# A one-layer hybrid trunk on one core: VectorE makes the last doubling of the scan's rotation, and GpSimd's pool sums wait twice

## The chip, the core and the metric

The kernel runs on one core of a Trainium2 chip. A core has five engines with queues of their own: TensorE (PE, matrix products into PSUM banks), VectorE (DVE), ScalarE (ACT), GpSimd (POOL), and SyncE (SP), which here only issues DMAs. They meet in semaphores: an instruction adds to one when it is done, and a queue can wait until one has reached a count. The metric is the device time of one execution in microseconds, lower is better.

## The reference

For 512 tokens of width 1024 (float32):

```
z = x @ w_in                       # split: pool 256, q k v 3 x 384, ssm 384
pool : mean of the last 2/4/8/16 tokens minus the token, per group @ w_pool, * pool_scale
attn : 6 heads of 64, causal by chunks of 64, clipped relative-position bias, softmax
ssm  : 24 groups of 16 channels, 64 complex states each:
       s[t] = abar * s[t-1] + bbar @ u[t];  y = Re(c @ s) + d * u
       y = gelu(y);  y = y * sigmoid(y @ w_glu + b_glu)      # the gated unit
h    = LayerNorm(alpha*x + concat(rmsnorm(pool), rmsnorm(attn), rmsnorm(ssm)) @ w_out)
ffn  = top-2 of 16 experts (silu(h@w_gate) * (h@w_up)) @ w_down, inside the best group of 4
ple  = sigmoid(h @ w_ple_gate) * (p @ w_ple_proj)
x    = LayerNorm(alpha*h + ffn + ple)
```

The change touches the state space group (ssm) and the pool group.

## The kernel before

The program is written out by hand, one queue for each engine; what stands in a queue runs in that order, and no scheduler moves anything. Many fp32 products are made as three products of rounded parts: an upper part (ScalarE copies into fp32r), and a lower part (VectorE or GpSimd subtracts the upper one). `xv_lo` (value input), `wv_lo` (value weights), `gelu_lo` and `wg_lo` (gated unit) are such lower parts.

**The scan.** The 512 tokens are cut into 64 chunks (NC) of 8 tokens. TensorE makes each chunk's contribution x (`products`, signal `pe_x`) into four PSUM banks, for 12 pairs of groups (Q) of 128 states by 64 chunks, real and imaginary. The complex scan over the chunks is made real by a rotation: VectorE multiplies x by the turned unit vectors `cosv` and `sinv` (L1697 to L1706), scans real and imaginary parts with the real decay (L1708), and rotates back (L1716 to L1721), which signals `s_ready`. The rotation table `rot` holds the powers 0 to 64 of a unit vector, and **GpSimd** makes it by doubling: with powers 1 to m at hand, powers m+1 to 2m are these times power m, a complex product of six instructions (L557 to L562), for m = 1, 2, 4, 8, 16, 32. Then it writes the decay array (L565, L566), which signals the third `rot_ready`, and VectorE waits for that.

**GpSimd's queue** goes on behind it: 16 DMA issues that put half of the matrix `m0` together (L575; SP issues the other half), the first running sums of the pool group (`add_shift`, L583 and L584), `xv_lo` in two subtractions (L594), and, once VectorE has put y and the skip term together (`yin_ready`), the longer sums, a multiply by the reciprocal counts (L602, `rcnt`) and a subtract of the token (L603), which signals `pool_ready`. For this TensorE's pool product (L1258), ScalarE's squares and one of SP's loads wait. `gelu_lo` is made by VectorE at L1758 (`glu_lo_set`, with the weights' part before it: 4 in all); TensorE's gated unit (L1219 to L1221) waits for all four, ScalarE's gates (L814) for it.

**VectorE's queue** around it: bias and row maximum of heads 0 and 1, the wait, the rotation and scan, `normalise(0)` and `normalise(1)` (a reciprocal, then four multiplies of a softmax block, L1676, signal `p_norm`), bias of heads 2 and 3 (L1656, L1658; for `scores(1)` of TensorE), their maxima (L1667), the same for heads 4 and 5, `wv_lo`, the other normalisations, then y (L1747), copies of transposed probabilities (`pt_move`, L1752) and `gelu_lo`. **TensorE's queue**: x, two q/k projections, half of the pool projection, scores(1), the first value tile, scores(2) (waits for the bias of heads 2 and 3, `s_read` 4), y, the second value tile (its second term takes `xv_lo`, its third `wv_lo`), transposes of the probabilities, more value tiles, the gated unit, the pool product, attention times values, the output product. **ScalarE** makes the exponentials (L767) and copies y out of PSUM (L822).

Of the kernel before, what the change touches and what calls it, by code (L numbers as in the profile page):

```python
# [23 lines left out]
P = 128  # L24
# [10 lines left out]
NC = T // CH  # L35
# [82 lines left out]
def trunk(nc, io, out):  # L118
    with ExitStack() as ctx:
# [384 lines left out]
        def _(gp):  # L504
            n = [0]

            def link(ins):

                n[0] += 1
                ins.then_inc(S["gp_step"], 1)  # L510
                gp.wait_ge(S["gp_step"], n[0])
# [25 lines left out]
            link(g.tensor_copy(rot[:, 0, :, 1:2], u8[:, 0, :].unsqueeze(2)))  # L537
            link(g.tensor_copy(rot[:, 1, :, 1:2], u8[:, 1, :].unsqueeze(2)))
            m = 1
            while m < NC:  # L540
                if m == 8:
                    gp.wait_ge(S["rb_in"], 16)
                    g.memset(rbias[0:64, :, 192:256], NEG).then_inc(S["rot_ready"], 1)
                    for i in range(4):
                        h, f = i % 2, i // 2
                        gp.dma_start(w_pl[64 * h:64 * h + 64, f, 64 * h:64 * h + 64], io["w_pool"][i]).then_inc(S["gp_in"], 16)
                    gp.dma_start(inv_d.rearrange("(p c) o -> p (c o)", p=P), pad_t[:]).then_inc(S["inv_put"], 16)
                    gp.wait_ge(S["pe_qk"], 4)
                    g.memset(m0, 0.0).then_inc(S["rot_ready"], 1)
                    gp.wait_ge(S["kern_in"], 4)  # L550
                shape = [P, Q, m]
                t = tmp_g[:, 0:Q * m].rearrange("p (q c) -> p q c", q=Q)
                ar, ai = rot[:, 0, :, 1:m + 1], rot[:, 1, :, 1:m + 1]
                br = rot[:, 0, :, m:m + 1].broadcast_to(shape)
                bi = rot[:, 1, :, m:m + 1].broadcast_to(shape)
                orr, oi = rot[:, 0, :, m + 1:2 * m + 1], rot[:, 1, :, m + 1:2 * m + 1]
                link(g.tensor_tensor(t, ai, bi, ALU.mult))  # L557
                link(g.tensor_tensor(orr, ar, br, ALU.mult))
                link(g.tensor_tensor(orr, orr, t, ALU.subtract))
                link(g.tensor_tensor(t, ar, bi, ALU.mult))  # L560
                link(g.tensor_tensor(oi, ai, br, ALU.mult))
                link(g.tensor_tensor(oi, oi, t, ALU.add))  # L562
                m *= 2
# [12 lines left out]

            gp.wait_ge(S["pool_in_done"], 2)
            gp.wait_ge(S["pe_x"], 1)
            a, b2 = pl_s[:, 0], pl_s[:, 1]

            def add_shift(o, i, w, lo, ms):
# [17 lines left out]
            link(g.tensor_copy(b2[64:P, 1:2], a[64:P, 1:2]))  # L599
            add_shift(a, b2, 8, 64, second)  # L600
            gp.wait_ge(S["rc_in"], 16)
            link(g.tensor_tensor(a, a, rcnt, ALU.mult))  # L602
            g.tensor_tensor(a, a, plT, ALU.subtract).then_inc(S["pool_ready"], 1)  # L603

# [922 lines left out]
        def _(dv):  # L1527
# [153 lines left out]
            row_max(0)  # L1681
            row_max(1)

            dv.wait_ge(S["pe_x"], 1)
            dv.wait_ge(S["rot_ready"], 3)
            half = Q // 2 * NC
            cosv, sinv = rot[:, 0, :, 0:NC], rot[:, 1, :, 0:NC]

            def qc(ap):
                return ap.rearrange("p (q c) -> p q c", c=NC)  # L1690
            for u in range(2):
                xr, xi = qc(bank[X_BANKS[0][u]][:, 0:half]), qc(bank[X_BANKS[1][u]][:, 0:half])
                cs, sn = cosv[:, 6 * u:6 * u + 6], sinv[:, 6 * u:6 * u + 6]
                cols = slice(u * half, (u + 1) * half)
                o_r, o_i = qc(x_rot[:, 0, cols]), qc(x_rot[:, 1, cols])
                t_r, t_i = qc(x_tmp[:, 0, cols]), qc(x_tmp[:, 1, cols])
                link(tt(o_r, xr, cs, ALU.mult))  # L1697
                link(tt(t_r, xi, sn, ALU.mult))
                link(tt(o_i, xi, cs, ALU.mult))
                last = tt(t_i, xr, sn, ALU.mult)  # L1700
                if u == 0:
                    link(last)
# [435 lines left out]
```

## Time and profile before

| | before |
|---|---|
| median of 3 runs | 423.56 us (422.49 to 425.38) |
| profiled execution, time | 422.09 us |
| its span | 420.3 us |
| PE busy | 407.8 us (97%) |
| DVE busy | 260.9 us (62%) |
| ACT busy | 143.8 us (34%) |
| POOL busy | 115.5 us (27%) |
| chain that ended last | PE 47%; DVE 29%; issue 11%; DMA 5%; POOL 4%; ACT 3% |

TensorE is busy nearly all the time, but in the first half by small pieces that wait on the other engines; the second half is the experts. The chain that ended last is read back from the last instruction, at each step to what released it. Idle time of an engine counts only where such a chain goes through it. The row of a timeline may merge several instructions of a line; then its length is that of all of them, and its shape that of the first.

### The profile page before, as it was taken

How to read it: one execution, taken by the hardware profiler on the slowest of the kernel's cores; microseconds unless marked ns; L12 is line 12 of the kernel's file. 1: busy time of each engine (PE TensorE's matmuls, PEld its weight loads, DVE VectorE, ACT ScalarE, POOL GpSimd, SP SyncE). 2: the span in 40 equal slices, each digit the busy share in tenths (PEclk: the TensorE clock that was granted, in tenths of full speed). 3: DMA queues.
4: the chain of work that ended last, by engine and by line, in shares of the span. 5: the costliest groups of instructions: out<-in, count | busy, mean ns of one | idle time of the engine just before them, and what ended most of it. 6: DMA issues, size and time to landing. Idle time of an engine off the chain costs nothing.

```text
span 420.3 us, 5727 instructions
## 1 busy us (share of the span) xinstructions
PE 407.8 (97%) x2213; PEld 246.0 (59%) x2213; DVE 260.9 (62%) x467; ACT 143.8 (34%) x254; POOL 115.5 (27%) x142
## 2 busy tenths in 40 slices
PE   8999999999999999999999999999999999999992
PEld 5767755459987557888587876333333333333281
DVE  2999994999884999999988323111110112224986
ACT  4732236248757891214520101011111011111284
POOL 2811258457054706000001640011101111000050
PEclk9999999999999999999999999999999999999998
DMA  7994103350579995111763239999999999978204
GB/s 269 430 403 139 50 2 62 74 131 27 132 294 343 397 409 202 50 51 50 271 281 105 95 85 387 423 394 423 420 419 419 417 412 409 423 279 299 101 13 188
DMA packets 33643, 102.77 MB, mean 245 GB/s; under 512 B 14898, under 2 KB 16098, under 8 KB 26832
## 3 DMA queue, kind: packets, MB, share of 16 engines
q1 hardware_dynamic: 26048, 92.79, 56.8%
q0 software_dynamic: 4016, 7.97, 5.6%
q10 hardware_dynamic: 3552, 1.65, 1.4%
q8 instruction: 18, 0.29, 0.3%
q14 instruction: 9, 0.07, 0.1%
HBM read 93.29 MB, written 15.24 MB: 258 GB/s over the span
## 4 chain that ended last, share of the span: by engine, by line
PE 47%; DVE 29%; issue 11%; DMA 5%; POOL 4%; ACT 3%; SPq 0%; DVEq 0%; POOLq 0%; ACTq 0%
PE bank L1392 20%; PE bank L1402 10%; DVE region_f L1812 4%; PE bank L1387 3%; PE bank L1227 3%; PE bank L1467 3%; PE bank L1143 2%; POOL slot_scratch L631 1%; DMA region_h<-y_scratch 1%; ACT region_a L767 1%; DVE ln_st L1815 1%; DVE region_a L1658 1%; DVE region_a L1676 1%; DVE att_mx L1667 1%; DMA region_h<-slot_scratch 1%
## 5 line engine op out<-in xcount | busy, mean ns | idle before, releaser
L1392 PE MATMUL bank<-region_a,region_g 128*64 128x512 f32 (+1 forms) x224 | 77.8, 594 | 0.0
L1974 DVE TENSOR_TENSOR region_c<-region_c,bank 128x256 f32<-128x256 f32 x12 | 5.1, 421 | 64.7 <-ACT region_c L962 64.7
L1402 PE MATMUL bank<-region_a,region_c 128*64 128x512 f32 (+1 forms) x160 | 43.7, 596 | 0.0
L1392 PE MATMUL bank<-region_h,region_g 128*64 128x512 f32 (+1 forms) x96 | 42.4, 594 | 0.0
L1392 PE MATMUL bank<-region_c,region_g 128*32 128x512 f32 (+1 forms) x96 | 42.4, 595 | 0.0
L1392 PE MATMUL bank<-region_b,region_g 128*64 128x512 f32 (+1 forms) x96 | 42.4, 594 | 0.0
L1967 DVE COPY region_g<-bank 128x512 f32<-128x512 f32 x24 | 15.4, 686 | 40.6 <-PE bank L1387 40.6
L1392 PEld LDWEIGHTS bank<-region_a,region_g 128*64 128x64 f32 (+1 forms) x224 | 22.2, 123 | 25.1 <-issue 24.4
L962 ACT ACTIVATE region_c<-bank 128x256 f32<-128x256 f32 x12 | 4.6, 384 | 83.9 <-PE bank L1392 83.9
L1013 PE MATMUL bank<-region_e,region_a 128*128 128x512 f32 x64 | 28.0, 595 | 0.0
L1320 PE MATMUL bank<-ple_gate_upper,hidden_upper 128*128 128x512 f32 x64 | 25.7, 402 | 0.0
L1322 PE MATMUL bank<-ple_gate_upper,hidden_lower 128*128 128x512 f32 x64 | 25.0, 390 | 0.0
L1321 PE MATMUL bank<-ple_gate_lower,hidden_upper 128*128 128x512 f32 x64 | 24.9, 389 | 0.0
L1402 PEld LDWEIGHTS bank<-region_a,region_c 128*64 128x64 f32 (+1 forms) x160 | 12.0, 123 | 22.1 <-issue 22.0
L644 POOL DMA_INDIRECT expert_scratch<-region_g,region_h x5 | 5.0, 1001 | 65.1 <-ACT region_g L945 65.1
L1402 PE MATMUL bank<-region_c 128*32 128x512 f32 (+1 forms) x48 | 21.9, 596 | 0.0
L1402 PE MATMUL bank<-region_b,region_c 128*64 128x512 f32 (+1 forms) x48 | 21.7, 595 | 0.0
L1013 PEld LDWEIGHTS bank<-region_e,region_a 128*128 128x128 f32 x64 | 12.0, 190 | 14.6 <-issue 14.3
L907 ACT ACTIVATE region_h<-bank 128x512 f32<-128x512 f32 x8 | 4.8, 598 | 41.8 <-PE bank L1322 30.3
L1392 PEld LDWEIGHTS bank<-region_h,region_g 128*64 128x64 f32 (+1 forms) x96 | 11.4, 123 | 12.5 <-issue 12.2
L1812 DVE SCALAR_TENSOR_TENSOR region_f<-bank,rms_r,region_f 128x512 f32<-128x512 f32 x24 | 18.0, 750 | 0.7
L631 POOL DMA_INDIRECT slot_scratch<-region_h,slot_i x8 | 8.2, 1027 | 36.4 <-issue 36.4
(380 smaller groups left out, 969.8 us busy)
## 6 DMA issues: line engine op xcount, KB each, us to landing
region_a<-in_w_exp_down SPq DMA_DIRECT2D x10, 1024.0 KB, 11.9
region_a<-in_w_exp_gate SPq DMA_DIRECT2D x7, 1024.0 KB
region_a<-in_w_exp_up SPq DMA_DIRECT2D x7, 1024.0 KB
expert_scratch<-zero_scratch SPq DMA_DIRECT2D x8, 512.0 KB, 13.7
region_b<-in_w_out SPq DMA_DIRECT2D x1, 3072.0 KB, 12.4
region_c<-in_w_ple_gate SPq DMA_DIRECT2D x2, 1536.0 KB, 12.0
region_b<-in_w_exp_gate SPq DMA_DIRECT2D x3, 1024.0 KB, 10.1
region_b<-in_w_exp_up SPq DMA_DIRECT2D x3, 1024.0 KB, 11.7
```

The lines of the kernel that those rows point to most:

```text
L631: gp.indirect_dma_start(out=inv_d, out_offset=bass.IndirectOffsetOnAxis(ap=slot_i[:, 2 * i + k:2 * i + k + 1], axis=0), in_=pair_i[:, 2 * ...
L1013: last = mm(bank[bank_i][:], w[:, k, m * P:(m + 1) * P], xT[:, k, :], start=(k == 0), stop=(k == KD - 1))
L1227: last = mm(bank[WO_AT[half][group]][:], hdT[:, k, t * P:(t + 1) * P], w_o[:, k, half * 512:half * 512 + 512], start=(i == 0), stop=(i == ...
L1320: mm(bank[PG_AT[k % 2]][:], h_hi[t][:, x], pg_hi[:, w], start=(c == 0), stop=False)
L1321: mm(bank[PG_AT[k % 2]][:], h_hi[t][:, x], pg_lo[:, w], start=False, stop=False)
L1322: last = mm(bank[PG_AT[k % 2]][:], h_lo[t][:, x], pg_hi[:, w], start=False, stop=(c == KD - 1))
L1387: last = nc.tensor.transpose(bank[B_TOK[k // 4]][:, (k % 4) * P:(k % 4 + 1) * P], hg[:, r, k:D:KD], ident[:])
L1392: return mm(out_[at:at + width].rearrange("p (u n) -> p u n", u=2), x[:, k, at:at + width], w[:, k], start=(k == 0), stop=(k == KD - 1), t ...
L1402: return mm(bank[banks[half]][at:at + width, :], act_e[:, r, 2, k * P + at:k * P + at + width], w[:, k, half * 512:half * 512 + 512], star ...
L1467: last = mm(bank[OH_BANKS[t][half]][:], onehot[i][:, t * P:(t + 1) * P], y[:, half * 512:half * 512 + 512], start=(t not in X_AT and i == ...
L1812: last = stt(xh[:, t, cols], bank[WO_AT[half_][group]][:], rms_r[:, group, t:t + 1], xh[:, t, cols], ALU.mult, ALU.add)
L1967: v.tensor_copy(hgT[:, t % 2, 4 * u:4 * u + 4, :], bank[B_TOK[u]][:].rearrange("p (k s) -> p k s", k=4)).then_inc(S["hgT_evac"], 1)
```

## The change

GpSimd's loop ends one doubling earlier (m = 16 is the last). VectorE makes the sixth, from powers 1 to 32 and power 32, right after its wait for `rot_ready`, with the helper `cmul`, which has the same six instructions; its scratch is `x_tmp`. Its wait for `pe_x` stands behind that now. GpSimd's first pool sums wait for two normalisations (`p_norm` 2) in addition, and its multiply by `rcnt` waits for all four lower parts of the gated unit (`glu_lo_set` 4).

```diff
@@ GpSimd
             m = 1
-            while m < NC:
+            while m < NC // 2:
@@
             gp.wait_ge(S["pool_in_done"], 2)
             gp.wait_ge(S["pe_x"], 1)
+            gp.wait_ge(S["p_norm"], 2)
             a, b2 = pl_s[:, 0], pl_s[:, 1]
@@
             gp.wait_ge(S["rc_in"], 16)
+            gp.wait_ge(S["glu_lo_set"], 4)
             link(g.tensor_tensor(a, a, rcnt, ALU.mult))
@@ VectorE
-            dv.wait_ge(S["pe_x"], 1)
             dv.wait_ge(S["rot_ready"], 3)
...
+            wide_ = [P, Q, NC // 2]
+            turn_r, turn_i = rot[:, 0], rot[:, 1]
+            at_r, at_i = (t_[:, :, NC // 2:NC // 2 + 1].broadcast_to(wide_) for t_ in (turn_r, turn_i))
+            cmul(turn_r[:, :, NC // 2 + 1:NC + 1], turn_i[:, :, NC // 2 + 1:NC + 1], turn_r[:, :, 1:NC // 2 + 1], turn_i[:, :, 1:NC // 2 + 1],
+                 at_r, at_i, x_tmp[:, 0, 0:Q * NC // 2].rearrange("p (q c) -> p q c", q=Q))
+            dv.wait_ge(S["pe_x"], 1)
```

On GpSimd, at the end of the rotation (region_f holds `rot` and the decay; L565 and L566 write the decay, L575 puts `m0` together), the six rows of the last doubling go:

```order
 L561 TENSOR_TENSOR region_f<-region_f 128x12x16 [waits gp_step]
 L562 TENSOR_TENSOR region_f<-region_f 128x12x16 [waits gp_step]
-L557 TENSOR_TENSOR region_f<-region_f 128x384 [waits gp_step]
-L558 TENSOR_TENSOR region_f<-region_f 128x12x32 [waits gp_step]
-L559 TENSOR_TENSOR region_f<-region_f 128x12x32 [waits gp_step]
-L560 TENSOR_TENSOR region_f<-region_f 128x384 [waits gp_step]
-L561 TENSOR_TENSOR region_f<-region_f 128x12x32 [waits gp_step]
-L562 TENSOR_TENSOR region_f<-region_f 128x12x32 [waits gp_step]
 L565 COPY region_f<-region_b 128x768 [waits gp_step]
 L566 MEMSET region_f 128x12 [waits gp_step]
```

The decay's copy follows the fifth doubling directly. On VectorE, after the row maxima of head 1 (L1669), the changed kernel has these rows (region_b holds `x_tmp` and the rotated x, bank the products x; L1704 is what L1697 was):

```order
L1669 TENSOR_REDUCE att_mx<-region_a 128x1 x3
L1541 TENSOR_TENSOR region_b<-region_f 128x384 [waits rot_ready]
L1542 TENSOR_TENSOR region_f<-region_f 128x12x32 [waits dve_step]
L1543 TENSOR_TENSOR region_f<-region_f,region_b 128x12x32 [waits dve_step]
L1544 TENSOR_TENSOR region_b<-region_f 128x384 [waits dve_step]
L1545 TENSOR_TENSOR region_f<-region_f 128x12x32 [waits dve_step]
L1546 TENSOR_TENSOR region_f<-region_f,region_b 128x12x32 [waits dve_step]
L1704 TENSOR_TENSOR region_b<-bank,region_f 128x384 [waits pe_x,dve_step]
```

The six products stand in front of the first rotation, and only that one waits for x. The two waits that GpSimd gains stand at the first pool sum and at the multiply by `rcnt`, in the changed kernel:

```order
L584 COPY region_c<-region_g 128x2 [waits p_norm,pe_x,pool_in_done]
L585 TENSOR_TENSOR region_c<-region_g 128x2x511 [waits gp_step]
L584 COPY region_c<-region_c 128x2 [waits gp_step]
L585 TENSOR_TENSOR region_c<-region_c 128x510 [waits gp_step]
L584 COPY region_c<-region_c 64x2 [waits gp_step]
L585 TENSOR_TENSOR region_c<-region_c 64x510 [waits gp_step]
L595 TENSOR_TENSOR value_input_lower<-region_e,value_input_upper_102 128x2560 [waits pe_v,xw_hi_set,gp_step]
...
L604 TENSOR_TENSOR region_c<-region_c 128x1024 [waits glu_lo_set,rc_in,gp_step]
L605 TENSOR_TENSOR region_c<-region_c,region_g 128x1024 [waits gp_step]
```

Nothing changes its place there; the first and the last but one row have one semaphore more to wait for, and xv_lo (L595) stands behind the first of the two waits.

## Rows read from the trace of the kernel before

**Rows 1.** the page of the profile, its first line

```profile
span 420.3 us, 5727 instructions
```

**Rows 2.** timeline of GpSimd (POOL); columns: start us, us, engine, line, operation, tiles, count, idle before

```profile
62.22 0.84 POOL L557 TENSOR_TENSOR region_f<-region_f 128x384 f32<-128x384 f32 x1
...
67.94 0.83 POOL L565 COPY region_f<-region_b 128x768 f32<-128x768 f32 x1
...
69.57 8.27 POOL L575 DMA_DIRECT2D region_h<-region_c  x16 [0.62 <-POOL region_f L566]
86.31 0.22 POOL L583 COPY region_c<-region_g 128x2 f32<-128x2 f32 x1 [8.48 <-ACT region_g L741]
```

**Rows 3.** timeline of VectorE (DVE), from the first softmax head to the third

```profile
59.86 2.71 DVE L1667 TENSOR_REDUCE att_mx<-region_a 128x1 f32<-128x384 f32 x6
69.05 0.56 DVE L1697 TENSOR_TENSOR region_b<-bank,region_f 128x384 f32<-128x384 f32 x1 [6.49 <-POOL region_f L566]
...
84.54 0.95 DVE L1721 TENSOR_TENSOR region_b<-region_b 128x756 f32<-128x756 f32 x1
...
85.61 1.28 DVE L1676 TENSOR_SCALAR region_a<-region_a,att_sm 128x128 f32<-128x128 f32 x4
...
87.01 3.48 DVE L1676 TENSOR_SCALAR region_a<-region_a,att_sm 128x128 f32<-128x128 f32 x4
...
97.24 0.60 DVE L1658 SCALAR_TENSOR_TENSOR region_a<-bank,region_f 128x128 f32<-128x128 f32 x2
```

**Rows 4.** timeline of TensorE (PE), 62 to 95 us

```profile
61.80 3.02 PE L1112 MATMUL bank<-region_h,region_c 128*64 128x64 f32 x96
...
85.55 2.43 PE L1085 MATMUL bank<-region_g 64*128 64x256 f32 x16
...
94.22 2.43 PE L1085 MATMUL bank<-region_g 64*128 64x256 f32 x16 [0.89 <-DVE region_a L1658]
```

**Rows 5.** timeline of ScalarE (ACT)

```profile
102.60 0.40 ACT L767 ACTIVATE region_a<-region_a,att_mx 128x128 f32<-128x128 f32 x1 [0.84 <-DVE att_mx L1667]
...
108.31 0.58 ACT L822 ACTIVATE region_b<-bank 128x512 f32<-128x512 f32 x1
```

**Rows 6.** timeline of VectorE, where y comes back

```profile
117.44 2.08 DVE L1747 SCALAR_TENSOR_TENSOR region_h<-region_h,vec 128x512 f32<-128x512 f32 x3 [3.11 <-DMA region_h<-y_scratch]
119.43 3.14 DVE L1752 COPY region_a<-bank 128x512 f32<-128x512 f32 x6
```

**Rows 7.** timeline of TensorE, from the value projection to the pool product

```profile
107.32 1.64 PE L1076 MATMUL bank<-value_weights_upper,value_input_upper 128*128 128x384 f32 x8
...
120.26 1.38 PE L1133 MATMUL bank<-ident,region_a 128*128 128x128 f32 x10 [0.74 <-DVE region_a L1752]
...
128.08 0.48 PE L1219 MATMUL bank<-gelu_upper,glu_upper 128*128 128x512 f32 x1
...
134.33 1.88 PE L1258 MATMUL bank<-region_c,w_pl 128*128 128x512 f32 x4
```

**Rows 8.** timeline of VectorE, an earlier complex product from SBUF to SBUF

```profile
25.54 0.76 DVE L1541 TENSOR_TENSOR region_b<-region_b 128x576 f32<-128x576 f32 x1
```

**Rows 9.** timeline of GpSimd, the pool sums and the value input's lower part

```profile
90.61 1.03 POOL L584 TENSOR_TENSOR region_c<-region_c 64x510 f32<-64x510 f32 x1
93.51 9.06 POOL L594 TENSOR_TENSOR value_input_lower<-region_e,value_input_upper 128x2560 fp32r<-128x2560 f32 x2 [1.86 <-PE bank L1061]
...
122.63 1.67 POOL L584 TENSOR_TENSOR region_c<-region_c 64x504 f32<-64x504 f32 x1
124.38 2.71 POOL L602 TENSOR_TENSOR region_c<-region_c 128x1024 f32<-128x1024 f32 x1
127.17 2.72 POOL L603 TENSOR_TENSOR region_c<-region_c,region_g 128x1024 f32<-128x1024 f32 x1
```

**Rows 10.** the line of gelu_lower on VectorE, its three instructions

```profile
L1758 DVE TENSOR_TENSOR gelu_lower<-region_h,gelu_upper x3: 676/1755/2871, 122.5 to 124.8; 128x512 fp32r<-128x512 f32 x3
```

**Rows 11.** timeline of ScalarE, the second gate

```profile
132.48 0.69 ACT L814 ACTIVATE region_h<-bank,vec 128x512 f32<-128x512 f32 x1 [1.35 <-PE bank L1221]
```

## The prediction

> **What bounds the kernel now.** I read the chain that ended last first, then the timelines of each engine between 55 and 135 us, where the change lies. The profiled execution has a span of 420.3 us [rows 1] and 422.09 us on the clock; the median of the three timed runs is 423.56 us, 1.5 us above it. The sum below is made against the profiled one, and its difference is then put on the median.
>
> The chain goes through GpSimd's rotation. VectorE is through with its two row maxima at 62.6 us and then idles 6.49 us, released by GpSimd's memset of the decay array [rows 3]; GpSimd spends 62.22 to 67.94 on the last doubling alone [rows 2]. But the idle is not all on the path. Behind it VectorE rotates x, scans, rotates back (s_ready at 85.49), normalises heads 0 and 1 (until 90.4), and adds the bias of heads 2 and 3. That last step also needs scores(1), which TensorE finishes at 87.98, at the end of an unbroken stretch of its own [rows 4]. TensorE then waits 0.89 us for VectorE before scores(2) [rows 4]. So VectorE's delay reaches TensorE, but TensorE was nearly there by itself: the value tile in front ended at 94.22 - 0.89 = 93.33. From there the path is VectorE's bias of heads 4 and 5 (from 97.24) [rows 3], their maxima, exponentials on ScalarE (102.60, after 0.84 us of waiting for the maxima), the third copy of y (108.31) [rows 5], two DMAs, VectorE at 117.44, its first probT copy, and TensorE at 120.26 after a wait of 0.74 us for it [rows 6, 7]. From 120.26 to 157 us TensorE runs on its own work, and what follows starts from its results.
>
> **The doubling moves.** GpSimd drops six multiply and add instructions, 67.94 - 62.22 = 5.72 us [rows 2]. Its decay copy starts at 62.22, and rot_ready comes 5.72 us earlier; VectorE starts at 69.05 - 5.72 = 63.33. It is free, since its maxima end at 62.57. It now runs the same six over 384 elements with both inputs in SBUF. No row has this size. The nearest are 0.76 us for 576 elements [rows 8] and 0.95 us for 756 [rows 3]; the line through them gives 0.57 at 384, which is also what the PSUM form of that size takes (0.56) [rows 3]. With the 0.02 to 0.03 us between linked instructions that is 0.59 us each, 3.54 us in all. The bounds are 0.59 and 0.79 us each, so 3.5 to 4.7 us; I take the lower, by the size. The new order asks for pe_x only after the six: products end at 64.82 [rows 4], so this costs nothing at 66.87.
>
> Rotation, scan and s_ready come 69.05 - 66.87 = 2.18 us earlier (1.0 at the upper bound): s_ready at 83.3. GpSimd's sixteen DMA issues of m0 start 5.7 us earlier and end at about 72.1 instead of 77.84 [rows 2]. Nothing of theirs is needed before the y products at 96 us, and SP's queue has its own copies of the other half. GpSimd's next work, the pool sums, waits for the pool projection's copy until 86.31 as before.
>
> **p_norm before the pool sums.** Before, normalisation of head 1 took 3.48 us for its four instructions, that of head 0 1.28 us [rows 3]; the difference of 2.2 us falls on the time in which GpSimd runs its first shifted sum from 86.31 on [rows 2]. After the move both normalisations follow s_ready: 83.43 to 84.7 and 84.8 to 86.05. They are done before GpSimd could start. So the new wait removes nothing that the doubling has not already removed, and costs GpSimd nothing: 86.05 against 86.31. Each of the two edits alone would clear this collision; together they don't add up. Queued behind the wait are the sums (86.31 to 91.64), then xv_lo, which waits for the first value tile and starts at 93.51 anyway, ending at 102.57 [rows 9]. TensorE wants xv_lo in the second term of the next value tile, one term of 1.5 us after 107.32 [rows 7]. So p_norm could come 1.8 us later than 86.31 without moving xv_lo, and xv_lo has 5 us more.
>
> **Where the 2.18 + 2.2 us stop.** VectorE would be ready for bias 2 at 86.1, 4.4 us earlier than now, but scores(1) ends at 87.98. It starts at 88.05 instead of 90.41, and idles 1.9 us in front. s_read 4 comes 2.36 us earlier, at 91.8, and TensorE goes from the value tile straight into scores(2) at 93.33: **0.89 us** gained there. Scores(2) takes 2.43 us and ends at 95.76; VectorE has its two maxima done by 94.9, so bias 4 starts at 95.85 instead of 97.31 (the chain's start, behind the maxima; the timeline's merged row says 97.24): **1.46 us**. Exponentials 4 start at 101.15, y copy 2 at 106.85. ScalarE is there in time, since the glu weights' DMA is issued behind the earlier s_ready. The y products end at 107.32 - 0.89 = 106.43, 0.4 us before, so they don't bind. The DMAs of y shift along, VectorE's 117.44 becomes 115.98, and the wait of 0.74 us before TensorE's 120.26 shrinks by the difference of 1.46 and 0.89, to 0.2. TensorE goes on about **1.4 us** earlier. If the doubling took its upper bound on VectorE, normalisation 1 would end at 87.2, still before scores(1): the same 1.4.
>
> **glu_lo_set before the last pool steps.** The three instructions of gelu_lower take 0.68, 1.76 and 2.87 us [rows 10]. The second and third end 0.55 us behind GpSimd's 64-partition sum (124.30) and its multiply by rcnt (127.09) [rows 9]. The Trainium skill's page "SBUF — State Buffer", section "Who interferes with whom", says that a VectorE instruction with two SBUF inputs contends with a GpSimd one that reads SBUF, and the later of the two waits out the whole of the other; the trace agrees. With the multiply held back, the third takes 0.68: glu_lo_set 4 comes at 127.64 - 1.4 - 2.2 = 124.0; without relief it would be 126.2. TensorE starts the gated unit at 128.08 now, behind its transposes, 0.4 us after the lower parts, so at 126.7 after the change. Both times are before it: this relief is worth 0. The cost: GpSimd's multiply and subtract (2.71 + 2.72 = 5.43 us) [rows 9] start at 124.0 to 126.2 and pool_ready is at 129.5 to 131.7, before 129.89. Behind it stand ScalarE after its second gate (133.2 now, 131.8 then) [rows 11], TensorE's pool product (134.33 now, 132.9 then) [rows 7], and SP's load of a gate weight half. All are reached later, so the wait costs nothing either; its cover is 0 to 2 us.
>
> **The sum.** 1.4 us, and no step further on pulls against it: the loads after 112 us are issued by events that move along, and the expert stage follows TensorE. Span 418.9; 422.09 - 1.4 = 420.7 for the profiled run; on the median 423.56 - 1.4 = 422.1 us.
>
> **Rivals.**
> (a) *The gain is given back* before the end, by one of the DMA queues or in the experts' gather: 423.6. For it: the loads from 112 to 150 us come back to back. Against it: every wait of TensorE's that I find from 120 to 157 us is its own work. Chance 0.09.
> (b) *All of VectorE's 2.2 us comes through*: 421.4. It would need TensorE to be free before 93.33, and its stretch from 64.8 has no gap. Or GpSimd's relief shortens something that the chain doesn't show. Chance 0.06.
> (c) *Slower: VectorE's six are blocked by GpSimd*, as gelu_lower was. At 1.76 us each [rows 10] the doubling takes 10.5 us, not 3.5, s_ready is at 90.3 and bias 2 at 93.0, 2.6 us later than 90.41: 426.2. It decides from 7.9 us for the six (1.3 each) upward. Against it: the same DMA issues lay beside VectorE's rotations at 69.6 to 77.8, and those ran at 0.56 us [rows 2, 3]. Chance 0.04. By the skill's same section such a tensor_tensor takes the shared read interface only and descriptors need the write interface (which it calls inferred), so by that page (c) doesn't happen; the trace agrees.
> (d) *pool_ready late*: from 131.8 on it holds up ScalarE's squares and gains are lost one for one; slower than before needs 133.2, with lower parts at 127.8, 1.6 us later than my unrelieved case. Price 1 us beyond that, 424.6. Chance 0.01.
>
> **How the numbers follow.** Likeliest, 1.4 us: 0.80, its own range 420.9 to 423.3, where the bounds of the terms (0.9, if y binds, to 2.2) are small beside the 2.9 us between the lowest and highest timed run. Range for all: 420.1 to 424.6, leaving out (c) and the tails of the measurement. Faster or slower by over 1% (4.2 us, about what a measurement of this kernel can tell from no change) is out of reach of all cases but the far end of (c): faster 0.03, same 0.94, slower 0.03.
>
> **What would show it.** Right: six VectorE instructions of 0.56 to 0.6 us from 63.3; s_ready at 83.3; normalisation 1 at 1.2 us with GpSimd's sums still starting at 86.3; a new idle of 1.9 us before bias 2, ended by TensorE; no wait of TensorE before scores(2); third gelu_lower at 0.7 us with TensorE's gated unit at 126.7; pool_ready before 131.8 with no wait on it. Wrong: a VectorE wait before y that grows, TensorE idle before the pool product, or a chain from 157 us on that is not a copy of the old one 1.4 us earlier.

## The result and the profile after

| | before | after |
|---|---|---|
| median, 6 runs each | 423.59 us (422.49 to 425.38) | 419.99 us (419.89 to 420.23) |
| profiled execution, time | 422.09 us | 420.23 us |
| its span | 420.3 us | 418.5 us |

The ratio of after to before is 0.9916, with a 95% interval of 0.9895 to 0.9937. The medians differ by 3.6 us where 1.5 were forecast, and 419.99 lies 0.1 us below the forecast range. One execution of the unchanged kernel (470.66 us) and one of the kernel with the glu wait alone (435.37 us) ran at a lower mean granted clock, 0.945 and 0.966, and are left out of every median and count below. Two things stand out in the table: the two profiled executions differ by only 1.8 us, half of what the medians do, and after's six times lie within 0.34 us where before's are 2.9 us apart.

The page of the profile of after, its first line and what its chain that ended last is made of:

```profile
span 418.5 us, 5727 instructions
...
PE 64%; DVE 18%; issue 11%; DMA 3%; ACT 2%; POOL 1%; DVEq 0%; POOLq 0%; ACTq 0%
```

TensorE's share of the chain has risen from 47% to 64%, VectorE's has fallen from 29% to 18%. The chain in order of time no longer passes through the rotation: TensorE's own work carries it from 61.5 us to the end of scores(2).

VectorE's timeline in after, with the columns of [rows 2]. L1541 to L1546 are the moved doubling, L1678 the two normalisations, L1660 the bias of heads 2 and 3 and then 4 and 5, L1754 is y, L1759 the probT copies and L1765 gelu_lower:

```profile
63.44 0.56 DVE L1541 TENSOR_TENSOR region_b<-region_f 128x384 f32<-128x384 f32 x1 [0.68 <-POOL region_f L566]
64.03 0.56 DVE L1542 TENSOR_TENSOR region_f<-region_f 128x384 f32<-128x384 f32 x1
...
67.00 0.56 DVE L1704 TENSOR_TENSOR region_b<-bank,region_f 128x384 f32<-128x384 f32 x1
...
82.49 0.94 DVE L1728 TENSOR_TENSOR region_b<-region_b 128x756 f32<-128x756 f32 x1
...
83.56 1.27 DVE L1678 TENSOR_SCALAR region_a<-region_a,att_sm 128x128 f32<-128x128 f32 x4
...
84.95 1.27 DVE L1678 TENSOR_SCALAR region_a<-region_a,att_sm 128x128 f32<-128x128 f32 x4
87.63 0.62 DVE L1660 SCALAR_TENSOR_TENSOR region_a<-bank,region_f 128x128 f32<-128x128 f32 x2 [1.41 <-PE bank L1087]
...
95.35 0.62 DVE L1660 SCALAR_TENSOR_TENSOR region_a<-bank,region_f 128x128 f32<-128x128 f32 x2 [0.80 <-PE bank L1087]
...
114.52 2.07 DVE L1754 SCALAR_TENSOR_TENSOR region_h<-region_h,vec 128x512 f32<-128x512 f32 x3 [2.06 <-DMA region_h<-y_scratch]
117.56 3.15 DVE L1759 COPY region_a<-bank 128x512 f32<-128x512 f32 x6 [0.97 <-PE bank L1135]
120.62 2.11 DVE L1765 TENSOR_TENSOR gelu_lower<-region_h,gelu_upper 128x512 fp32r<-128x512 f32 x3
```

The six products run from 63.44 to 67.0 at 0.56 us each. s_ready is at 83.4 (against 85.5), the normalisations take 1.27 us each and end at 86.2, and bias 2 waits 1.41 us for scores(1). These rows answer to [rows 3, 6].

GpSimd's and TensorE's timelines in after:

```profile
86.39 0.19 POOL L584 COPY region_c<-region_g 128x2 f32<-128x2 f32 x1 [14.09 <-DVE region_a L1678]
...
93.12 9.04 POOL L595 TENSOR_TENSOR value_input_lower<-region_e,value_input_upper 128x2560 fp32r<-128x2560 f32 x2 [1.84 <-PE bank L1063]
...
122.90 2.38 POOL L604 TENSOR_TENSOR region_c<-region_c 128x1024 f32<-128x1024 f32 x1 [1.92 <-DVE gelu_lower L1765]
125.36 2.40 POOL L605 TENSOR_TENSOR region_c<-region_c,region_g 128x1024 f32<-128x1024 f32 x1
...
85.16 2.43 PE L1087 MATMUL bank<-region_g 64*128 64x256 f32 x16
...
92.88 2.43 PE L1087 MATMUL bank<-region_g 64*128 64x256 f32 x16
...
118.39 1.38 PE L1135 MATMUL bank<-ident,region_a 128*128 128x128 f32 x10 [0.22 <-DVE region_a L1759]
...
126.20 0.48 PE L1221 MATMUL bank<-gelu_upper,glu_upper 128*128 128x512 f32 x1
...
132.46 1.88 PE L1260 MATMUL bank<-region_c,w_pl 128*128 128x512 f32 x4
```

GpSimd's sums start at 86.39, behind the normalisations, and xv_lo at 93.12, released by TensorE as before [rows 9]. Its multiply at 122.90 waits 1.92 us for gelu_lower, and pool_ready is at 127.8. TensorE goes into scores(2) at 92.88 without a wait (0.89 us in [rows 4]), waits 0.22 us for its first probT copy (0.74 in [rows 7]), and starts the gated unit at 126.20 and the pool product at 132.46 (128.08 and 134.33). So 1.9 us separate the two traces. Of these, 0.4 us lie ahead of the change: scores(1) starts at 85.16 instead of 85.55, because TensorE's first twelve products of the program took 5.42 us in this execution and 6.69 in the other. What is left of the pair is 1.5 us, the forecast. The other half of the measured gain isn't in this pair of traces. If it was real, it was in executions of before that hadn't been profiled.

### The profile page after: what moved, and what is told of

The parts are those of the page before. It is cut to its first block, busy times and chain, and to the rows that moved or that the text cites. A ratio compares the mean times of both kernels' runs of the same rounds, so it can differ in the third digit from the quotient of the medians.

```text
span 418.5 us, 5727 instructions
## 1 busy us (share of the span) xinstructions
PE 406.8 (97%) x2213; PEld 245.4 (59%) x2213; DVE 259.6 (62%) x473; ACT 143.8 (34%) x254; POOL 108.6 (26%) x136
## 4 chain that ended last, share of the span: by engine, by line
PE 64%; DVE 18%; issue 11%; DMA 3%; ACT 2%; POOL 1%; DVEq 0%; POOLq 0%; ACTq 0%
PE bank L1394 20%; PE bank L1404 10%; PE bank L1015 7%; DVE region_f L1819 4%; PE bank L1389 3%; PE bank L1078 3%; PE bank L1229 3%; PE bank L1469 3%; PE bank L1087 2%; PE bank L1145 2%; PE bank L1135 2%; POOL slot_scratch L633 1%; PE bank L1202 1%; PE bank L1063 1%; PE bank L1203 1%
```

## The experiments

Two theories stood against each other. *Two collisions*: executions of before mostly lose more at the places where VectorE and GpSimd meet (the normalisations beside the pool sums, gelu_lower beside the multiply by rcnt) than the profiled one did. *Something else*: the profiled pair shows all there is, and the rest comes from the chips or from elsewhere in the program. All comparisons are with before on the same chip.

**The kernel before, unchanged, profiled again.** No edit.

> The kernel before, unchanged, for more of its executions and a second trace. Theory A (a lottery of locks): the executions of the kernel before that take 423.6 us and more lose 1.5 us or more against the profiled one of 422.09 in a stretch where GpSimd and VectorE collide, so a second trace with a longer time shows a longer normalisation of head 1 or a longer gelu_lower, and TensorE waiting for it. Theory B (start-up): the spread comes from the first 50 us (arrival of the first loads, the clock's rise), and the collisions last as long in this trace as in the first: 3.48 us for the four normalisation instructions and 1.76 and 2.87 us for gelu_lower. Both expect 422 to 425.5 us, ratio 1.000.

Median 423.45 us (422.26 to 425.61), ratio 0.9998 (0.9975 to 1.0021). The trace differs from the first one. TensorE's and GpSimd's timelines:

```profile
87.26 2.43 PE L1085 MATMUL bank<-region_g 64*128 64x256 f32 x16
...
129.49 0.50 PE L1219 MATMUL bank<-gelu_upper,glu_upper 128*128 128x512 f32 x1 [0.94 <-DVE gelu_lower L1758]
...
88.03 0.48 POOL L583 COPY region_c<-region_g 128x2 f32<-128x2 f32 x1 [9.99 <-ACT region_g L741]
```

The twelve first products took 8.04 us here, so scores(1) came at 87.26 and GpSimd's sums at 88.03, 1.7 us later than in [rows 2, 4]. VectorE had its normalisations done by then, at 1.27 us each, and nothing waited before scores(2). But gelu_lower took 6.71 us for its three instructions, and TensorE waited 0.94 us for it before the gated unit. Same code, another loss at another place. This trace is 1.4 us slower than the first, with a longer gelu_lower and TensorE waiting for it, as the first of the two theories asked.

**The doubling alone** (after without its two new waits):

```diff
-            gp.wait_ge(S["p_norm"], 2)
-            gp.wait_ge(S["glu_lo_set"], 4)
```

> Only the move of the last doubling, no new waits. The prediction's theory: it carries the whole gain, so 1.4 us below before in a profile of equal start, and the same 420.0 us as the full change. Theory A: normalisation 1 no longer collides (it is over at 86.1), but gelu_lower still does, so this kernel keeps a spread of over 1 us between its executions and a median of 421 to 422.5, above the full change.

Median 421.15 us (420.78 to 421.40), ratio 0.9932 (0.9906 to 0.9958): 2.5 us below before. The normalisations take 1.27 us each, TensorE has no wait before scores(2), and 0.76 us before the gated unit, behind a gelu_lower of 6.52 us. So the doubling gave 2.5 us where 1.4 were forecast, and a loss at gelu_lower is left.

**The norm wait alone** (before with it):

```diff
             gp.wait_ge(S["pool_in_done"], 2)
             gp.wait_ge(S["pe_x"], 1)
+            gp.wait_ge(S["p_norm"], 2)
```

> Only GpSimd's wait for two normalisations, the doubling stays on GpSimd. The prediction's theory: normalisation 1 shrinks from 3.48 to 1.3 us, bias 2 starts at 88.3 us instead of 90.4, TensorE goes on 1.2 to 1.4 us earlier: as much as the doubling alone gives; GpSimd's sums move to 88.3 to 93.6 and xv_lo hardly moves. Ratio 0.997. Theory A: more than that if the collision at the normalisation is what costs before its 1.5 us; then close to 420.5 us.

Median 420.77 us (420.65 to 421.66), ratio 0.9935 (0.9912 to 0.9958): 2.9 us below before, from one semaphore. TensorE's and GpSimd's timelines:

```profile
92.83 2.43 PE L1086 MATMUL bank<-region_g 64*128 64x256 f32 x16
...
119.07 1.38 PE L1134 MATMUL bank<-ident,region_a 128*128 128x128 f32 x10 [0.97 <-DVE region_a L1753]
...
126.88 0.48 PE L1220 MATMUL bank<-gelu_upper,glu_upper 128*128 128x512 f32 x1
...
88.53 0.19 POOL L584 COPY region_c<-region_g 128x2 f32<-128x2 f32 x1 [10.62 <-DVE region_a L1677]
```

GpSimd's sums start 2.2 us later than in [rows 2], and nobody misses them. Scores(2) at 92.83 has no wait. What the later s_ready still costs shows at 119.07, where TensorE waits 0.97 us for the first probT copy.

**The glu wait alone** (before with it):

```diff
             gp.wait_ge(S["rc_in"], 16)
+            gp.wait_ge(S["glu_lo_set"], 4)
```

> Only GpSimd's wait for the gated unit's lower parts. The prediction's theory: worth 0, since TensorE reaches the gated unit 0.4 us after the lower parts as it is; ratio 1.000, 423.6 us. Theory A at this place: the 0.4 us of cover is gone in the executions over 422.1 us, where gelu_lower ends behind TensorE's transposes, so this kernel is at 421.5 to 422.3 us with a smaller spread.

Median 423.46 us (422.31 to 424.16), ratio 0.9989 (0.9969 to 1.0009): no gain, and the 421.5 to 422.3 us of the collision theory did not come. Up to 117 us this is the code of before, and its trace shows the collision of the normalisations in its worst form. VectorE's, GpSimd's and TensorE's timelines, then the stretches of 1 us (the granted clock is the third number from the end):

```profile
85.88 2.92 DVE L1677 TENSOR_SCALAR region_a<-region_a,att_sm 128x128 f32<-128x128 f32 x4
...
88.92 2.63 DVE L1677 TENSOR_SCALAR region_a<-region_a,att_sm 128x128 f32<-128x128 f32 x4
...
86.00 0.21 POOL L583 COPY region_c<-region_g 128x2 f32<-128x2 f32 x1 [7.88 <-ACT region_g L742]
...
95.28 1.13 PE L1086 MATMUL bank<-region_g 64*128 64x256 f32 x5 [2.26 <-DVE region_a L1659]
...
96.00:97.00 1.00, 1.00 (x6) 0.52 (x6) 1.00 (x4) 0.62 (x3) 1.00 (x1) 0.73 0.00 0
97.00:98.00 1.00, 1.00 (x7) 0.90 (x6) 1.00 (x3) 0.94 (x5) 1.00 (x1) 0.50 0.05 16
98.00:99.00 1.00, 1.00 (x7) 0.68 (x4) 0.52 (x2) 0.97 (x3) 1.00 (x2) 0.50 0.00 0
99.00:100.00 1.00, 1.00 (x7) 1.00 (x7) 1.00 (x5) 0.97 (x5) 1.00 (x1) 0.57 0.00 0
100.00:101.00 1.00, 1.00 (x12) 1.00 (x10) 1.00 (x5) 0.97 (x3) 1.00 (x1) 1.00 0.00 0
```

TensorE's first products took 5.42 us in this execution, so GpSimd's first sum began at 86.00, while VectorE was in its first normalisation, and both normalisations were drawn out: 2.92 and 2.63 us, together 5.55, against 4.76 in [rows 3] and 2.54 without a collision. TensorE, which was early too, waited 2.26 us before scores(2) instead of 0.89. Behind that wait its granted clock was 0.73 and then 0.50, the 1.2 GHz level, until shortly before 100 us, and scores(2) took 3.52 us instead of 2.43. Further on the wait did what it was added for: gelu_lower took 1.94 us, and TensorE reached the gated unit without a wait. Of the 11 executions this one alone has a mean clock below 0.993.

**The doubling and the glu wait** (after without the norm wait):

```diff
-            gp.wait_ge(S["p_norm"], 2)
```

> The full change without GpSimd's wait for the normalisations. The prediction's theory: with the doubling on VectorE both normalisations end at 86.2 us, before or within 0.2 us of the time at which GpSimd's sums start, so that wait is worth nothing: 420.0 us, the same as the full change. Rival: the sums start at 85.9 in most executions and block the last instruction of head 1's normalisation by up to 1 us; scores(1) still ends later than that, so it costs nothing either, but where both slip it would show as executions of 421 us and more.

Median 420.05 us (419.13 to 420.70), ratio 0.9909 (0.9882 to 0.9937), span 418.4: the same as after. GpSimd's sums start at 85.94 as VectorE is in its last 0.27 us of normalisation, and both normalisations take 1.27 us. Beside the doubling the norm wait is worth nothing, as predicted.

**The doubling and the norm wait** (after without the glu wait):

```diff
-            gp.wait_ge(S["glu_lo_set"], 4)
```

> The full change without the wait for the gated unit's lower parts. Theory L: y comes back early, so that GpSimd's multiply starts before the second instruction of gelu_lower; the three take 6.5 us, TensorE waits 0.8 us before the gated unit, 421.1 us as with the doubling alone. The prediction's theory (that wait is worth 0): 420.0 us.

Median 421.14 us (420.54 to 421.33), ratio 0.9932 (0.9906 to 0.9958): 1.1 us above after, which was forecast as 0. VectorE's, GpSimd's and TensorE's timelines:

```profile
120.60 6.42 DVE L1764 TENSOR_TENSOR gelu_lower<-region_h,gelu_upper 128x512 fp32r<-128x512 f32 x3
...
120.98 2.72 POOL L603 TENSOR_TENSOR region_c<-region_c 128x1024 f32<-128x1024 f32 x1
...
118.38 1.38 PE L1134 MATMUL bank<-ident,region_a 128*128 128x128 f32 x10 [0.22 <-DVE region_a L1758]
...
127.07 0.50 PE L1220 MATMUL bank<-gelu_upper,glu_upper 128*128 128x512 f32 x1 [0.62 <-DVE gelu_lower L1764]
```

GpSimd's multiply starts at 120.98, 0.4 us behind gelu_lower. The three instructions take 0.85, 2.85 and 2.87 us, 6.42 from first to last where 5.15 was seen in before, and TensorE waits 0.62 us for them at 127.07. The gated unit starts 0.87 us later than in after. The span differs by 0.9 us.

**Both waits, the doubling left on GpSimd** (before with both):

```diff
+            gp.wait_ge(S["p_norm"], 2)
...
+            gp.wait_ge(S["glu_lo_set"], 4)
```

> Both waits, the doubling stays on GpSimd. Theory L (the time of before is set by which of the two engines comes first at two places, and the waits alone take both collisions away): no wait of TensorE before scores(2) nor before the gated unit, and 0.97 us of waiting for the first probT copy as in the kernel with the normalisation wait alone: 420.7 us, so that the doubling is worth 0.7 us of the 3.6. The prediction's theory, in which the doubling carries the gain: above 421 us.

Median 420.85 us (420.42 to 421.84), ratio 0.9937 (0.9913 to 0.9961). So the doubling, the part with most code in it, is worth about 0.8 us once the waits are there (420.85 against 420.05 in the same session; the intervals of the two ratios overlap a little). The trace shows where: TensorE's wait before the first probT copy is 0.78 us here and 0.22 in after. ScalarE's third copy of y is 1.4 us later than in after (107.81 against 106.44), and y's way through memory 0.5 us longer. The glu wait is worth nothing here: the norm wait alone stands at 420.77 us, and in its trace gelu_lower took 5.15 us and TensorE still didn't wait for it.

**The kernel before, a third and a fourth time.** No edit, one profiled execution each.

> The kernel before once more, for a third trace. Theory L: if TensorE's first products run at the pace of the kernels with a new wait (12 of them in 5.4 us), GpSimd's sums start at 86.0 us, within the normalisation of head 0, both normalisations take 5.5 us together, TensorE waits 2.3 us before scores(2), and the time is 424 to 425.5 us. If those products take 8 us, the sums start at 88.0, nothing collides there, and the time is 423.4 us.

421.90 us. It repeats the first trace: twelve products 6.65 us, normalisations 1.28 and 3.48, 0.95 us before scores(2), nothing before the gated unit.

> The kernel before once more, in search of the trace of an execution of 425 us. Theory L: if the time is above 424.5 us, TensorE waits 2.3 us before scores(2) and 0.8 us before the gated unit, both in one execution; if it is 423.5 us, it has one of the two.

424.83 us, span 423.1. TensorE's timeline, and two of its stretches of 1 us:

```profile
85.01 2.43 PE L1085 MATMUL bank<-region_g 64*128 64x256 f32 x16
...
95.03 1.64 PE L1085 MATMUL bank<-region_g 64*128 64x256 f32 x6 [2.24 <-DVE region_a L1658]
...
130.72 0.50 PE L1219 MATMUL bank<-gelu_upper,glu_upper 128*128 128x512 f32 x1 [0.50 <-DVE gelu_lower L1758]
...
97.00:98.00 1.00, 1.00 (x9) 0.92 (x5) 1.00 (x3) 0.94 (x4) 1.00 (x1) 0.50 0.07 16
98.00:99.00 1.00, 1.00 (x6) 0.76 (x5) 0.69 (x4) 0.97 (x3) 1.00 (x2) 0.50 0.00 0
```

Here both losses and the clock come together: 2.24 us of waiting before scores(2), about 1.7 us of clock behind it (turn_probs(2) starts 3.78 us later than in after; the early start gives 0.15 back, the wait takes 2.24, and 1.69 are left), and 0.50 us before the gated unit, whose start is 4.5 us later than in after. The span is 4.6 us longer, of which these items make 4.3.

**Before with a later start** and **after with a later start.** Five more warm-up products in front of the first real one, which add work and leave out nothing. They were meant to bring TensorE 2 us late to the collision.

```diff
-            for _ in range(7):
+            for _ in range(12):
```

> The kernel before with twelve warm-up products instead of seven at the head of TensorE's queue, so that its first real product starts 2 us later while VectorE's and GpSimd's early work stays. Theory L: GpSimd's sums start at 88 us, behind both normalisations, which then take 1.28 us each; TensorE does not wait before scores(2); so the later start costs far less than 2 us, 423 to 424 us, 1.0 of before, and the executions of 425 us are gone if they come from this collision. Without theory L, a TensorE that is busy 97% of the span and starts 2 us later gives 425.6 us.

> The full change with the same twelve warm-up products. Theory L: nothing collides in this kernel, so the later start is paid in full where TensorE has no wait left: 420.0 + 2.0 - 0.2 (its last wait, before the transposes) = 421.8 us. If it is paid in full here and not in the kernel before, the spread of before comes from the order of arrival and not from the start itself.

Before with it: 426.57 us (424.76 to 427.81), ratio 1.0054 (1.0030 to 1.0078). After with it: 423.73 us (422.35 to 424.59), ratio to before 0.9990 (0.9970 to 1.0009). In before with the later start the premise failed in the profiled execution. TensorE's timeline:

```profile
5.67 5.32 PE L1023 MATMUL bank<-region_e,region_a 128*128 128x512 f32 x12
...
85.07 2.43 PE L1085 MATMUL bank<-region_g 64*128 64x256 f32 x16
...
95.10 1.13 PE L1085 MATMUL bank<-region_g 64*128 64x256 f32 x5 [2.24 <-DVE region_a L1658]
...
97.00:98.00 1.00, 1.00 (x11) 0.86 (x9) 1.00 (x3) 0.94 (x5) 1.00 (x1) 1.00 0.05 16
...
250.00:300.00 50.00, 47.77 (x277) 22.48 (x277) 11.37 (x20) 5.56 (x9) 8.37 (x9) 0.97 0.95 377
```

The first twelve real products start later, at 5.67 us, but take 5.32 us, so that scores(1) is early (85.07), the collision is at its worst, and TensorE waits 2.24 us. The granted clock stayed at 1.00 behind that wait. It fell at another place: TensorE waited 2.24 us for gathered rows at 253.70 (0.40 us for the same in before), and from 254 to 257 us the clock was 0.50, the only fall inside this execution. In after the premise held: the products start at 6.60, scores(1) at 86.28, and 1.1 us passes through in full, since TensorE has no wait left there that could take it up. Both kernels also lose about 1.8 us between the last scatter into the experts' slots and what reads it back, near 240 us, and I can't explain that. It makes the medians of the two unfit for the question, and both missed what was expected of them (423 to 424, and 421.8). The two traces show no more than this: in after a lateness of TensorE is paid in full, and in before TensorE was early after all and the collision as bad as in the glu wait alone.

**The glu wait with TensorE kept busy** (before with the glu wait and eight products that nothing reads, ahead of scores(2)):

```diff
+            gp.wait_ge(S["glu_lo_set"], 4)
...
+            for _ in range(8):
+                mm(bank[7][:, 0:P], ones[:], ones[:], start=True, stop=True)
             pe.wait_ge(S["s_read"], 4)
             scores(2)
```

> The kernel with the gated unit's wait alone, and eight dummy products of 128x128 (0.24 us each, 1.9 us) in TensorE's queue between the first value tile and scores(2), where that kernel waited 2.26 us and its granted clock then was 0.5 for 3.3 us. Clock theory: TensorE has work through most of the wait, the clock stays at 1.0 from 96 to 100 us, and the executions lie at 422.3 to 422.9 us (where the wait is only 0.9 us, the dummies cost 1.0 us themselves), a median 0.6 us or more below the 423.46 us of the kernel without dummies. Without it (the wait costs only its own length): the median stays at 423.5 us or rises by up to 1 us.

Median 424.26 us (422.67 to 426.03), ratio 1.0000 (0.9980 to 1.0021): the median did not fall, which is what was expected if the wait costs only its own length. TensorE's timeline, one stretch, and VectorE's wait for y:

```profile
92.72 1.95 PE L1191 MATMUL bank<-ones 128*128 128x128 f32 x16
95.12 1.13 PE L1086 MATMUL bank<-region_g 64*128 64x256 f32 x5 [0.46 <-DVE region_a L1661]
...
97.00:98.00 1.00, 1.00 (x12) 0.85 (x9) 1.00 (x3) 0.94 (x5) 1.00 (x1) 1.00 0.00 0
...
122.11 1.38 PE L1134 MATMUL bank<-ident,region_a 128*128 128x128 f32 x10 [1.69 <-DVE region_a L1755]
...
119.29 1.41 DVE L1750 SCALAR_TENSOR_TENSOR region_h<-region_h,vec 128x512 f32<-128x512 f32 x2 [4.07 <-DMA region_h<-y_scratch]
```

With 1.95 of the 2.4 us filled, TensorE starts scores(2) at 95.12, no earlier than without the products, and the clock stays at 1.00. Its pass up to 119.17 us is 1.8 us quicker than in the glu wait alone (120.94). But y comes back only at 119.29, after 4.07 us of VectorE waiting for the transfer, and TensorE waits 1.69 us at 122.11. ScalarE's third copy of y is 1.0 us earlier than in the glu wait alone (109.21 against 110.23); from there to VectorE y took 10.1 us through memory instead of 8.1, and that ate up the saving. Near 240 us this execution lost another 0.9. So this trace met something that neither alternative had: y's way isn't a constant. None of the 12 executions has a mean clock below 0.994. But only one of the 11 without the products had one below 0.993, so the experiment can't show that the products spared the clock, nor what that is worth in the median.

**What the times themselves say.** Every execution has its mean granted clock beside its time. The unchanged kernel ran 86 times in the four sessions of experiments. In 27 of them the mean clock is 0.992 or lower, and their times are 424.71 to 425.70 us. In the other 59 it is 0.993 or more, with 421.90 to 424.49 us and a median of 423.31. The two groups don't overlap. The fourth trace, with a mean of 0.989, shows the fall between 96 and 100 us; where it lay in the other 26 isn't recorded. The mean can't tell: in every trace the clock is at 0.50 in the last 3 to 6 us too, and the trace of before with the later start has its 0.992 from a fall at 254 us. In after with the later start, where nothing collides, 7 of 10 executions are at 0.992. In 39 executions of after and of the five kernels above in which the normalisations are clear of the sums (doubling alone, norm wait alone, and the three pairs), none has a mean clock below 0.993, and the times are 419.13 to 421.84 us.

| same code up to the normalisations | first 12 products | next product starts | GpSimd's sums start | normalisations | wait before scores(2) | before gated unit | span |
|---|---|---|---|---|---|---|---|
| before | 6.69 us | 11.05 | 86.31 | 1.28 + 3.48 | 0.89 | 0 | 420.3 |
| before, third | 6.65 | 10.99 | 86.23 | 1.28 + 3.48 | 0.95 | 0 | 420.2 |
| before, again | 8.04 | 12.78 | 88.03 | 1.27 + 1.27 | 0 | 0.94 | 421.7 |
| before, fourth | 5.42 | 10.20 | 85.78 | 2.91 + 2.63 | 2.24, clock 0.50 | 0.50 | 423.1 |
| glu wait alone | 5.42 | 10.77 | 86.00 | 2.92 + 2.63 | 2.26, clock 0.50 | 0 | 422.4 |
| glu wait filled | 6.19 | 10.62 | 85.86 | 2.92 + 2.63 | 0.46 behind 1.95 of filling | 0 | 423.0 |

VectorE's s_ready stands at 85.5 to 85.8 in all of them, while GpSimd's sums come from TensorE's pool projection and move with TensorE: they start 75.2 to 75.6 us behind the product that follows the first twelve, in all six. So the end of TensorE's first products goes with who of the two arrives first. In these traces an earlier TensorE has the worse collision at the normalisations. This order was seen and not set: the later start, which was to set it, did not. The change takes both meetings away, and with them most of the difference between one execution and the next (0.34 us in after's six; 1.6 us without the norm wait).

## Why the prediction was wrong, point by point

**The six products** (0.59 us each, bounds up to 0.79): 0.59 us from start to start, VectorE's first at 63.44 where 63.33 was forecast. (The line through the forecast's two rows gives 0.56 at 384 elements, not 0.57, which changes nothing.) Right, as was s_ready (83.4 against 83.3).

**The normalisations**: both at 1.27 us and over before the sums. Right, and that each edit alone would clear this collision is shown by the doubling alone and the norm wait alone; that they don't add up by the doubling and the glu wait, which equals after.

**The wait before scores(2)** ("0.89 us gained there") is the first step that failed. The mechanism was right, the wait is gone; its size was read from one execution, and of the six traces in the table only one lost less there. The third shows 0.95 us; the others show 2.24, 2.26 and 2.4 us (0.46 and the filling), or none beside a start 1.7 us later. With the doubling alone the kernel gained 2.5 us, not 1.4. In the text I saw that this execution was 1.5 us quicker than the median, and put the difference on the median as if the two differed by something that the change doesn't touch. In the fourth execution of before the same step costs 2.24 us and another 1.69 of clock. The Trainium skill's page "SBUF — State Buffer", section "Who interferes with whom", says that the order of issue, not the shape of the operation, decides who blocks. The table above fits it: four instructions of the same shapes took 1.27, 2.63, 2.92 or 3.48 us, depending on when GpSimd's sums started. The prediction applied that section to gelu_lower, where the later of the two waits, and didn't ask what an order other by half a microsecond would cost at the normalisations.

**Bias 4 and y** ("1.46 us earlier", y at 115.98): bias 4 at 95.35 instead of 95.85, y at 114.52 instead of 115.98. Of the 2.9 us that y gained, 0.4 is the start, 1.5 was forecast, and 1.0 is y's own way through memory: 8.1 us from ScalarE's copy to VectorE in after, 9.1 in before. The prediction took that way as fixed. Over the fourteen traces it is 8.0 to 10.1 us: where it is 8.3 or less, TensorE waits the same 0.22 us for its first probT copy, and VectorE itself waits for TensorE there (0.97 us before 117.56); where it is 8.6 or more, TensorE waits 0.67 to 1.69. In the five kernels with the doubling on VectorE it is 8.03 to 8.34, in the others 8.04 to 10.08.

**The glu wait** ("this relief is worth 0") failed as well. I moved gelu_lower and GpSimd's multiply by one and the same amount, so that their overlap stayed at 5.15 us. They moved differently. GpSimd follows y (its multiply is at 120.98 without the wait, 3.4 us earlier than in [rows 9]), gelu_lower the probT copies (1.9 us earlier), so that without the wait GpSimd's multiply holds up gelu_lower's second instruction and its subtract the third: 6.42 and 6.52 us, and TensorE waits 0.62 and 0.76. The wait is worth 1.1 us (421.14 against 419.99 and 420.05). It isn't only the change that makes this so: two of the four traces of before have a wait of 0.50 or 0.94 us there too.

**pool_ready** (between 129.5 and 131.7, not waited for): at 127.8, earlier since gelu_lower took 2.11 us; TensorE went into the pool product straight from the gated unit. Right that it costs nothing.

**TensorE 1.4 us earlier, then a copy of the old chain**: in the profiled pair 1.5 without the start, and from VectorE's first step of the sum over the groups (155.5 us; 157.4 in before) to the end of the span 263.0 us, against 262.9 in before. Right.

**The rivals.** (a), a gain given back, did not happen, (c), blocked doublings, did not (0.56 us each), nor did (d). (b) was nearest in its number, 421.4, and had the words "GpSimd's relief shortens something that the chain doesn't show", but not the mechanism. **The range** ended at 420.1: the largest saving I allowed was 2.2 us, which gives 421.4 from the median, and the rest was the spread of the timed runs. Its widest term should have been what the collision costs when GpSimd starts 0.5 us earlier.

**How the 3.6 us are made up**, as far as the runs carry it. By kernels, the doubling alone gives 2.5 us where 1.4 were forecast, and the glu wait beside it 1.1 where 0 was. By executions: against an execution of before in which the clock fell (median 425.2) after is 5.2 us quicker, and the fourth trace's span is 4.6 longer: 2.24, 1.69, and 0.50 at the gated unit, less 0.15 of an earlier start, make 4.3 of them. Against the others (median 423.3) it is 3.3 us quicker. Taking the clock's 1.69 away from the fourth trace leaves 2.9, which is an estimate: no run sets the clock's part apart. **Open** are four things. I have no trace of an execution of the unchanged kernel with a wait of 2.24 us and a full clock; that most of the 59 are of this kind was not shown, only that such a wait is in the trace with the later start (95.10). That the 27 lose the clock at scores(2) was shown for one of them. Why y's way through memory takes 8.0 us in one execution and 10.1 in another isn't settled, and why TensorE's first twelve products take 5.3 to 8.0 us wasn't tried.

No version was quicker than after; after without its norm wait is its equal, and before with only the norm wait is 2.9 us below before for one line.

## What to carry to other kernels

Where two engines hold each other up, a loss in one trace is one draw: before pricing it, profile several executions, and put the times of all runs beside it. If a profiled execution is quicker than the median by as much as the gain you expect, ask what differs, not how to scale it. A semaphore on the engine that has slack, here ahead of GpSimd's pool sums, cost nothing and removed the loss and most of the spread, and by itself it was worth as much as moving the work (420.77 and 421.15 us). What a wait is worth depends on what stands beside it: GpSimd's second wait gave 1.1 us with the doubling moved, and nothing beside the first wait alone.

## What the runs showed of the hardware

TensorE's granted clock went to 0.50, its 1.2 GHz level, after waits of 2.24 and 2.26 us before scores(2), for some 3 us (fourth trace of before and glu wait alone). In the trace of before with the later start it stayed at 1.00 after a wait of 2.24 us at the same place, and went to 0.50 from 254 to 257 us after another wait of 2.24 us. With 1.95 us of the wait before scores(2) filled by products that nothing reads it stayed at 1.00. So at one and the same wait the clock falls in some executions only. The mean clocks put it at 27 of 86 for the unchanged kernel, if the fall is at this place in all of them, which they can't show.

One and the same VectorE subtract (128x512) took 0.68 us alone and 2.85 to 2.90 us beside GpSimd's multiply or subtract of 2.7 to 2.8 us (gelu_lower in after, and in the second and fourth traces of before).

The first twelve products of the program, which wait for x and the first weights, took between 5.42 and 8.04 us in kernels that are alike up to there (5.32 and 5.78 with five more products ahead of them). The read-back behind the last scatter came 1.8 us later, beyond the later start, in both kernels with five more products in the first microseconds, for a reason that no run shows.
